# Hybrid decoder step: the down projection in five rounds, with the products stationary and 512 weight columns moving for six of the nine token tiles

## The reference, cut to what matters

```python
def conv_ffn(h, buf, w_gate, w_up, conv_w, conv_b, w_down):
    T = h.shape[1]
    a = h @ w_gate
    ext = jnp.concatenate([buf.astype(a.dtype), a], axis=1)
    c = conv_b + sum(conv_w[j] * ext[:, j:j + T] for j in range(CONV_W))
    y = (jax.nn.silu(c) * (h @ w_up)) @ w_down
    return y, ext[:, -(CONV_W - 1):]
...
        y, cbuf_p = conv_ffn(rms_norm(xp, norm2_g[l]), buf0, w_gate[l], w_up[l], conv_w[l], conv_b[l], w_down[l])
        xp = xp + y
```

## Time and profile before

| | |
|---|---|
| median of 3 runs | 1492.93 us (1491.44 to 1494.18) |
| the profiled execution, its own time | 1496.59 us |
| its span, first to last instruction | 1494.8 us |
| PE busy, PE weight loads busy | 1440.0 us, 1366.9 us |
| DVE, ACT, POOL busy | 879.7, 718.6, 664.7 us |
| granted TensorE clock, mean | 0.979 |
| down stage (first matmul to last transpose) | 1225.2 to 1490.1 us |

### The profile page before, as it was taken

One profiled execution on the slowest core, in us unless ns is written; L12 is line 12 of the kernel. 1 busy time (PEld: TensorE's weight loads), 2 busy tenths in 40 slices (PEclk: granted clock), 3 DMA queues, 4 the chain that ended last, 5 costly groups with the idle time before them and its releaser, 6 DMA issues.

```text
span 1494.8 us, 26853 instructions
## 1 busy us (share of the span) xinstructions
PE 1440.0 (96%) x10118; PEld 1366.9 (91%) x10118; DVE 879.7 (59%) x1453; ACT 718.6 (48%) x1378; POOL 664.7 (44%) x452
## 2 busy tenths in 40 slices
PE   7999999999999998989979999999999999999998
PEld 5888989798979887769979999999999999999998
DVE  6458545854585448756597776666666675614400
ACT  6537544745564455354464444444434444534432
POOL 0000300030003001322258888888888857666663
PEclk8999989998999899999999999999999999999999
DMA  8221103110311031845312122222122238857642
GB/s 273 94 66 29 43 17 101 35 38 17 101 43 30 17 100 39 245 149 167 119 44 82 46 74 86 86 86 82 62 86 86 86 124 289 255 168 232 212 137 67
DMA packets 160498, 153.67 MB, mean 103 GB/s; under 512 B 7959, under 2 KB 132508, under 8 KB 160412
## 3 DMA queue, kind: packets, MB, share of 16 engines
q1 hardware_dynamic: 159454, 152.24, 33.0%
q10 hardware_dynamic: 958, 0.26, 0.1%
HBM read 116.73 MB, written 35.74 MB: 102 GB/s over the span
## 4 chain that ended last, share of the span: by engine, by line
PE 52%; DVE 3%; issue 1%; ACT 0%; DVEq 0%; ACTq 0%
PE f_up L2234 9%; PE f_up L2236 9%; PE f_up L2235 9%; PE f_gp L2234 7%; PE f_gp L2236 7%; PE f_gp L2235 7%; PE f_dn L2234 1%; PE f_dn L2236 1%; PE f_dn L2235 1%; DVE room L2703 0%; DVE f_b22l L2713 0%; DVE f_t2f L2694 0%; DVE f_t L2711 0%; DVE f_b21l L2713 0%; DVE f_t1f L2689 0%
## 5 line engine op out<-in xcount | busy, mean ns | idle before, releaser
L2214 POOL TENSOR_TENSOR f_qlo<-f_braw,f_qhi 128x512 fp32r<-128x512 f32 x132 | 174.7, 1327 | 95.4 <-ACT f_qhi L2518 95.4
L143 PE MATMUL z_ps<-h_hi,w_hi 128*128 128x352 f32 x600 | 205.4, 342 | 0.0
L145 PE MATMUL z_ps<-h_hi,w_lo 128*128 128x352 f32 x600 | 197.3, 329 | 0.0
L144 PE MATMUL z_ps<-h_lo,w_hi 128*128 128x352 f32 x600 | 197.1, 328 | 0.0
L2210 POOL TENSOR_TENSOR f_qlo<-f_raw,f_qhi 128x512 fp32r<-128x512 f32 x88 | 154.0, 1759 | 34.5 <-ACT f_qhi L2493 34.5
L578 POOL TENSOR_TENSOR room<-room 128x1056 f32<-128x1056 f32 x4 | 9.7, 2433 | 330.6 <-ACT room L1235 330.6
L2518 ACT ACTIVATE f_qhi<-f_braw 128x512 fp32r<-128x512 f32 x132 | 83.3, 631 | 129.7 <-PE f_gp L2236 67.0
L2210 POOL TENSOR_TENSOR f_qlo<-f_sum,f_qhi 128x512 fp32r<-128x512 f32 x66 | 111.6, 1698 | 28.6 <-ACT f_qhi L2493 28.6
L143 PEld LDWEIGHTS z_ps<-h_hi,w_hi 128*128 128x128 f32 x600 | 116.7, 195 | 1.8 <-issue 1.3
L144 PEld LDWEIGHTS z_ps<-h_lo,w_hi 128*128 128x128 f32 x600 | 117.2, 195 | 0.3
L145 PEld LDWEIGHTS z_ps<-h_hi,w_lo 128*128 128x128 f32 x600 | 116.4, 194 | 0.0
(11 more groups left out here) (453 smaller groups left out, 4806.8 us busy)
## 6 DMA issues: line engine op xcount, KB each, us to landing
f_braw<-w_down SPq DMA_DIRECT2D x132, 256.0 KB, 3.5
w_raw<-w_in SPq DMA_DIRECT2D x28, 512.0 KB, 4.0
a_d<-f_u SPq DMA_DIRECT2D x11, 1056.0 KB, 7.0
f_stage<-a_d SPq DMA_DIRECT2D x66, 176.0 KB, 3.6
f_raw<-w_gate SPq DMA_DIRECT2D x22, 512.0 KB, 5.0
f_raw<-w_up SPq DMA_DIRECT2D x22, 512.0 KB, 5.2
room<-x_d SPq DMA_DIRECT2D x6, 1408.0 KB, 8.0
room<-x_prompt SPq DMA_DIRECT2D x8, 512.0 KB, 7.3
```

What stands on the lines that cost most here:

```text
L143: nc.tensor.matmul(out, whi[:, k, :], hi[:, k, :], start=(k == 0), stop=False)
L144: nc.tensor.matmul(out, whi[:, k, :], lo[:, k, :], start=False, stop=False)
L145: last = nc.tensor.matmul(out, wlo[:, k, :], hi[:, k, :], start=False, stop=(k == chunks - 1))
L2214: tt(qlo[q % ITEMS][:, :, :], braw[q % 8][:, :, :], qhi[q % ITEMS][:, :, :].bitcast(F32), ALU.subtract).then_inc(aw_ready, 1)
```

## The change

There are five rounds. The tokens are cut differently: 512 first (tiles 0 to 3), and the other 544 (`REST`).

| round | what is computed | a quad's 12 matmuls |
|---|---|---|
| 0, 1 | tiles 0 to 3, output channels 0-511, then 512-1023 | 12 with products stationary and 512 weight columns moving |
| 2, 3 | tiles 4 and 5 by 512 channels; tiles 6 to 8 (288 tokens) by two chunks of 128 channels | 6 with 512 columns, 6 with the weights stationary and 288 token columns moving |
| 4 | tiles 6 to 8 by the other four chunks (2, 3, 6, 7) | 12 with 288 columns |

Where the products are stationary, the sums come out in token rows. So for tiles 0 to 5 the residual is turned instead of the sums: before quad f = 8 of rounds 0 to 3 PE transposes the residual of the round's tiles into the idle set of banks (`turn_residual`), ACT copies it to `ybuf` at f = 10 and after, and at the end of the round DVE adds the banks to `ybuf`, from where it is stored. The tail's sums (tiles 6 to 8) are turned as before, half in round 4 before f = 8, half at the end.

Products are loaded 512 tokens wide for rounds 0 and 1, and 544 wide for the rest, and the latter are split in round 1. The residual's second and third parts are loaded in round 0, at q = 9 and q = 14. Round 4 loads weights as two pieces of 1 KB for each partition, before one of 2 KB.

```diff
-ROUNDS = 2 * NPC
+ROUNDS = 5
...
-                    sp.dma_start(braw[q % 8][:, :, :], d_view[f, r % 2]).then_inc(braw_in[q % 8], 16)
+                    if r < 4:
+                        sp.dma_start(braw[q % 8][:, :, :], d_view[f, r % 2]).then_inc(braw_in[q % 8], 16)
+                    else:
+                        sp.dma_start(braw[q % 8][:, :, :].rearrange("p (h k) c -> p h (k c)", h=2), last_view[f]).then_inc(braw_in[q % 8], 16)
...
                         acts_in(0, q + 5)
-                    if r % 2 and r < ROUNDS - 1:
-                        acts_in(r // 2 + 1, f)
-                        if f == 4:
-                            residual_back(r // 2 + 1)
-                    if r and f == 12:
+                    if q == 9:
+                        residual_back(1)
+                    if q == 14:
+                        residual_back(2)
+                    if r == 1:
+                        acts_in(1, f)
+                    if r and f == 6:
                         outputs(r - 1)
...
+                def turn_residual(r):
+                    pe.wait_ge(be_ready, KH * r)
+                    pe.wait_ge(r_in[0], 16)
+                    pe.wait_ge(r_in[1], 16)
+                    if r == 0:
+                        pe.wait_ge(c12_ready, 2 * MATS)
+                        pe.wait_ge(c21u_ready, 2 * GROUPS)
+                    if r >= 2:
+                        pe.wait_ge(r_in[2], 16)
+                    for s, y in enumerate(y_of(r)):
+                        t = Y_TILES[y][1]
+                        for j in range(KH):
+                            last = nc.tensor.transpose(sets[(r + 1) % 2][s][:, j * P:(j + 1) * P], acc[:, KH * (r % 2) + j, t * P:(t + 1) * P], keep["ident"][:, :])
+                        last.then_inc(yt_ready, 1)
...
                 for q in range(B_QUADS):
                     r, f = divmod(q, FC)
-                    n = r // 2
-                    if r and f == 4:
-                        turn_outputs(r - 1, sets[(r - 1) % 2], False)
+                    if r < 4 and f == 8:
+                        turn_residual(r)
+                    if r == 4 and f == 8:
+                        pe.wait_ge(be_ready, KH * 4)
+                        turn_tail((0, 1, 4, 5), 0)
...
                     for j in range(KH):
-                        triple(sets[r % 2][j][:, 0:PW], qhi[q % ITEMS][:, j, :], qlo[q % ITEMS][:, j, :], acts[f][0][:, :], acts[f][1][:, :],
-                               f == 0, f == FC - 1).then_inc(b_ready, 1)
-                pe.wait_ge(ye_ready, y_count(ROUNDS - 1))
-                turn_outputs(ROUNDS - 1, sets[0], True)
+                        if r < 2 or (r < 4 and j < 2):
+                            tile = slice(j * P, (j + 1) * P)
+                            ins = triple(sets[r % 2][j][:, :], ah[:, tile], al[:, tile], wh[:, :, :].rearrange("p k c -> p (k c)"),
+                                         wl[:, :, :].rearrange("p k c -> p (k c)"), f == 0, f == FC - 1)
+                        else:
+                            d = j - 2 if r < 4 else j
+                            ins = triple(sets[r % 2][j][:, 0:REST - 2 * P], wh[:, d, :], wl[:, d, :], ah[:, 2 * P:REST], al[:, 2 * P:REST],
+                                         f == 0, f == FC - 1)
+                        ins.then_inc(b_ready, 1)
+                pe.wait_ge(ye_ready, TURNED + len(TAIL))
+                for j, d in enumerate((2, 3, 6, 7)):
+                    pe.wait_ge(be_ready, KH * 4 + j + 1)
+                    turn_tail((d,), j)
...
                 def evict(r, j):
...
+                    if r < 2 or (r < 4 and j < 2):
+                        y = y_of(r)[j]
+                        dve.wait_ge(ye_ready, y + 1)
+                        v.tensor_tensor(ybuf[y % YBUFS][:, :], ybuf[y % YBUFS][:, :], sets[r % 2][j][:, :], ALU.add).then_inc(yd_ready, 1)
```

More of the change, by code:

```diff
@@ L1896, with y_of, act_slot @@
 L_SLOTS = {(1, 2): (0,), (1, 3): (1,), (1, 4): (2,), (1, 5): (3,), (2, 1): (4,), (2, 2): (5,), (2, 3): (6,), (2, 4): (7,), (2, 6): (8,), (2, 7): (9,)}
[L1899 to L1905, removed]
+def y_of(r, early=True):
+    return [y for y, (k, t) in enumerate(Y_TILES) if k == r and (r < 4 or (y < TURNED + len(TAIL)) == early)]
+def act_slot(f):
+    if f < 13:
+        return B11_AT + 2 * REST * f
+    if f < 18:
+        return PV_AT + 2 * REST * (f - 13)
+    return B22_AT + 2 * REST * (f - 18) if f < 21 else SUM_AT
 def p_use(m, i, z):
@@ L2354, in _ @@
                         matrix(g * 2 + b, g, b, False)
[L2356 to L2363, removed]
-                            last.then_inc(yt_ready, 1)
[L2365 to L2372, removed]
+                def turn_residual(r):
[8 more added lines that the diff above has]
+                    for s, y in enumerate(y_of(r)):
+                        t = Y_TILES[y][1]
+                        for j in range(KH):
+                            last = nc.tensor.transpose(sets[(r + 1) % 2][s][:, j * P:(j + 1) * P], acc[:, KH * (r % 2) + j, t * P:(t + 1) * P], keep["ident"][:, :])
+                        last.then_inc(yt_ready, 1)
@@ new lines, in turn_tail @@
+                def turn_tail(chunks, c):
+                    for s, t in enumerate(TAIL):
+                        w = P if t < NT else NS
+                        for d in chunks:
+                            last = nc.tensor.transpose(sets[1][s][0:w, c * P:(c + 1) * P], acc[:, d, t * P:t * P + w], keep["ident"][:, :])
+                            c += 1
+                        c -= len(chunks)
+                        if c + len(chunks) == KH:
+                            last.then_inc(yt_ready, 1)
@@ L2659, in _ @@
                         act_high(0, q + 6)
[L2660 to L2663, removed]
+                    if r == 1:
+                        act_high(1, f)
+                for s in (0, 2):
+                    turned(y_of(4, False)[s], sets[1][s])
                 act.wait_ge(conv_stored, 64 * GROUPS)
@@ L2869, in _ @@
                 for r in range(ROUNDS):
+                    if r == 0:
+                        for n in range(NPC):
+                            dve.wait_ge(r_in[n], 16)
                     for j in range(KH):
                         evict(r, j)
[L2872 removed]
+                    if r == 0:
                         for f in range(FC):
[L2874 to L2881, removed]
+                            act_low(1, f)
+                y = y_of(4, False)[1]
+                dve.wait_ge(yt_ready, y + 1)
+                dve.wait_ge(y_stored[y % YBUFS], 16 * (y // YBUFS))
+                v.tensor_copy(ybuf[y % YBUFS][:, :], sets[1][1][:, :]).then_inc(yd_ready, 1)
 def rel_bucket(n):
```

104 lines of the change are left out of this document (63 added, 41 removed).

## The result

| | before | after |
|---|---|---|
| median | 1492.72 us (10 runs) | 1498.88 us (10 runs) |
| ratio to before, 95% interval | | 1.0042 [1.0026, 1.0059] |
| span of the profiled execution | 1494.8 us | 1498.2 us |
| start of the first down matmul | 1225.24 us | 1222.87 us |
| from there to the end, "the stage" | 269.57 us | 275.33 us |

Forecast was 1494.4 us, with a range from 1488.6 to 1498.0. The change is slower, and lies outside the range.

What follows compares the result with a forecast made beforehand. PE alone was taken to bound the down stage. The terms -3.0 + 3.0 + 1.7 + 0.2 + 0.4 - 0.8 gave +1.5 us, so 1494.4 us, no change that can be told; range 1488.6 to 1498.0.

Steps and rivals of the forecast that it cites:

- Bound by PE alone: Down stage: PE alone sets the time, so only matmul intervals and waits put into PE's program count.
- The wait in round 0: Before quad 8 of round 0, PE idles 1.5 to 4.3 us for the second residual part; +3.0 us taken.
- The clock: Behind the idle stretch in round 0, PE runs at half speed for 3.3 us, costing +1.7 us.
- The matmuls: All five rounds: 264 fewer matmuls, same columns, each saving a fixed part of 11.5 ns; -3.0 us.
- Small terms: Start +0.2 us for a wider first product, body +0.4 for four more transposes, end -0.8 for fewer transposes and stores.
- Edits at nothing: POOL, ACT and DVE work, weight and product loads, additions and stores stay hidden under PE's quads, costing nothing.
- Slower: Rival, PE's queue in all rounds: columns alone set matmul time, so the gain vanishes; 1497.5 us, chance 0.30.
- The residual is there in time: Faster rival, round 0: PE does not wait and the clock stays, -3.2 us; 1489.7 us, chance 0.21.

Runs made afterwards that it cites:

- late_turn: The kernel with the change, but round 0's residual is turned before quad 14 instead of 8, ACT's copies moved along; 1489.28 us, 0.9971 of the kernel before.
- filler: The kernel with the change, plus 28 unused matmuls of 512 columns before the wait of quad 8, keeping PE busy; 1497.79 us, 1.0033 of the kernel before.
- late_again: late_turn unchanged, run once more on another chip job; 1491.61 us, 0.9965 of the kernel before.
- weights_still: late_turn with weights stationary and 512 tokens moving in rounds 0 and 1, outputs of tiles 0 to 3 not the reference's; 1488.88 us, ratio 0.996.
- halves: late_turn with each matmul of rounds 0 and 1 split into two of 256 columns on the same weights; 1494.12 us, 1.0012 of the kernel before.
- run 5: The run halves: late_turn with each 512-column matmul of rounds 0 and 1 split into two of 256; 1494.12 us.
- Experiment 6: The run weights_still: late_turn with weights stationary and tokens moving in rounds 0 and 1; 1488.88 us.

## Why the prediction was wrong, step by step

- **Bound by PE alone.** Right. late_turn changes no byte and no engine's work, and 8.75 us come back.
- **The wait in round 0: the step that failed.** Place and cause were right: one stretch, before L2391, for the second residual part, issued 3.2 us after quad 4 (2.6 to 3.3 foreseen). PE came to it 8.4 us after that end (8.3 foreseen). What failed is "it lands 7.2, 8.2 or 9.3 us after its issue". It took 12.5 us. I took a duration from rows where no second load of that size was in the queue, and carried it to a place where one was issued 5.7 us ahead. I named the first part as queued in front and put no price on it. 4.3 of the 4.5 us by which the wait was forecast too short are this. The 12.5 us are the upper end of what this place gives: with the same loads issued before it, at the same step, it landed after 11.1, 11.1, 11.4, 11.4 and 12.5 us in late_turn, filler, late_again, weights_still and halves. All lie above the 9.3 that I had as the worst. Why they differ among themselves stays open.
- **The clock: +1.7 foreseen, +2.0 measured.** The stretch at 0.50 was 6.8 us long, not 3.3, but 2.7 of it lay in the idle time. That the cost came out near is luck.
- **The matmuls: -3.0 foreseen, -3.6 measured in after and -2.9 in late_turn.** The sum was near, the reason was not, and that is luck. At 3.3 ns fixed, 264 matmuls fewer are worth 0.9 us. The rest is in pace, as far as it can be worked out: the 162.2 ns at 352 columns lie 0.8 above the line of run 5 (3.3 + 0.449 x 352 = 161.4), x 1584 = 1.3 us, and in rounds 2 to 4 of late_turn the distances lie below that line (231.7 ns for 233.2 at 512 columns, 132.1 for 132.6 at 288), 0.7 us. No run has 352 columns in the same places, so this split is argued, not shown. Taking the fixed part from two widths in two stages gave 11.5 because the stages differ by more than width. Of the forecast distances, 230.7 and 134.8 ns, after has 232.1 and 131.7: the wide ones cost 1.1 us more, the narrow ones 1.6 us less, and the second lies just outside the 132 to 136 given.
- **Small terms.** Start +0.25 (0.2 foreseen). Transposes: four more in the body and four fewer at the end, 7.34 us either way. What follows the last transpose became 0.11 us shorter. So the end was worth -0.55, not -0.8.
- **Edits at nothing.** Right: from 1257 us to the end PE has no idle stretch, and round 4 runs at 131.6 ns where POOL's 1.28 us were to fit into 1.62.
- **The rivals.** "Slower" came true in sign, but by another mechanism than the rival of that name. Its condition was met, a fixed part under 6 ns (3.3). It had the gain vanish with it, and the gain was there. "The residual is there in time" was the faster rival at 1489.7 us. late_turn makes it true and gives 1489.3 and 1491.6, where the kernel before had 1494.4 and 1494.2. The long wait had no rival of its own, and its upper end stood at 4.3 us, which is why the range ended at 1498.0.

Working backwards: with 12.5 us for the landing, the sum of the prediction would be 1.5 + 4.3 + 0.3 for the clock = +6.1 us. Measured: 6.0 in the trace.

The change keeps its gain if the residual is turned at quad 14. That version beats both kernels: 3.0 us under the kernel before in the stage, 2.7 with the 0.25 us ahead of it, in two executions, and 0.9971 and 0.9965 in the ratio, with intervals that end at 0.9998 and 0.9986. It is a small gain. Experiment 6 points to a further 2 us. A kernel that does so and turns the sums instead of the residual was not tried.

## What to carry to other kernels

The landing time of a load is a property of the queue at the moment of issue. Take it from a row only if the bytes in front are the same; otherwise add up what was issued before it and divide by the rate of the busy window. A wait placed by hand costs nothing to move as long as its result is not yet needed: put it as late as the consumer allows. Where the opening of a kernel varies by more than the effect, compare the stage from its own first instruction.

## What the runs showed of the hardware that was not expected

- A load of 1.44 MB took 7.5 to 12.5 us in one kernel. The part that took 12.5 us behind another of its size issued 5.7 us ahead took 7.5 us when issued 12.5 us behind it, at the same 378 or 379 GB/s.
- In after and with the load at q = 7 and 11, the loads that SP issued from the first residual part to the second landed in the order of their issue.
- The clock fell inside the longer idle stretches, not behind them. So in the 7.3 and the 8.7 us of idle time; with 3.3 us idle it fell 1.0 us after PE had gone on. It stayed at half for 3.4, 6.8 and 10.2 us, for 3.3, 7.3 and 8.7 us idle, and cost 1.6, 2.0 and 2.9 us in work. At half clock 512 columns took 427 ns, which is 512 / 1.2 GHz.
- The same 512 columns took 233.3 ns with the products stationary and 229.2 with the weights stationary.
- The same code ran rounds 3 and 4 at two paces. 512 columns in round 3 took 231.0 ns in after and 230.8 with the load at q = 11, and 234.4 or 234.5 in the others; round 4 took 131.6 ns a matmul against 132.7. That makes most of the 0.8 us between -3.6 and -2.9. Only the two runs with the longest waits show the faster pace; what sets it stays open.
